# Block 0's residual kept in DRAM through five MLP chunks, with accumulating transfers; down panels not kept split; weight sums spread

## The reference, cut to what matters

```python
h = x + mixed(rms_norm(x)) @ w_out          # RG-LRU and pooling, one input and one output projection
v = rms_norm(h, g_ffn)
up = causal_dwconv(v @ w_up, w_conv_ffn, b_conv_ffn)   # 1024 -> 6144, three taps
gate, val = up[..., :D_FF], up[..., D_FF:]
h = h + (gelu(gate) * val) @ w_down                    # 3072 -> 1024
q = rms_norm(h, g_ple)
h = h + sigmoid(q @ w_ple_gate + b_ple_gate) * (p @ w_ple_proj)
return rms_norm(h, g_final)
```

## Time and profile before

| | us |
|---|---|
| median of three runs | 2188.56 |
| lowest and highest | 2187.64 and 2188.94 |
| the profiled execution | 2192.39 |
| its span | 2190.5 |
| TensorE (PE) busy | 2108.1 |
| VectorE (DVE) busy | 1552.4 |
| ScalarE (ACT) busy | 909.1 |
| GpSimd (POOL) busy, issuing transfers | 396.4 |

### The profile page before, as it was taken

How to read it: one execution, slowest core, us unless ns; L and a number is a source line. 1 busy time by engine, 2 the same in 40 slices (tenths; PEclk the granted TensorE clock), 3 DMA queues, 4 the chain that set the end, 5 groups by cost and what they waited for, 6 DMA issues and landing times.

```text
span 2190.5 us, 24516 instructions
## 1 busy us (share of the span) xinstructions
PE 2108.1 (96%) x9152; PEld 1726.8 (79%) x9152; DVE 1552.4 (71%) x1823; ACT 909.1 (42%) x1194; POOL 396.4 (18%) x720
## 2 busy tenths in 40 slices
PE   8998999898999999898999999999999999999996
PEld 6877877786877778786788888888888888888885
DVE  7884398888888887888888662865555656564866
ACT  5663365253544445354553550641313132323342
POOL 0232322121211111121010010012211111122100
PEclk9999999999999999999999999999999999999998
DMA  5787978766666666668535253556666666666643
GB/s 218 240 235 281 300 239 261 249 238 230 262 230 231 246 245 258 246 237 307 215 107 179 90 204 97 172 174 195 193 192 193 193 194 195 195 193 192 210 155 106
DMA packets 141525, 460.00 MB, mean 210 GB/s; under 512 B 16608, under 2 KB 16736, under 8 KB 139104
## 3 DMA queue, kind: packets, MB, share of 16 engines
q0 software_dynamic: 93120, 350.27, 47.5%
q1 hardware_dynamic: 45984, 99.77, 14.1%
q10 hardware_dynamic: 2304, 8.39, 1.0%
HBM read 279.06 MB, written 204.47 MB: 221 GB/s over the span
## 4 chain that ended last, share of the span: by engine, by line
issue 39%; PE 31%; DVE 16%; POOL 7%; DMA 3%; ACT 2%; SPq 0%; POOLq 0%; DVEq 0%; ACTq 0%
PE slot L788 16%; PE slot L642 15%; POOL wpair L627 7%; DVE H L1874 4%; DVE wpair L1489 3%; DMA raw<-panels 1%; DMA split_panels<-wpair 1%; ACT wpair L923 1%; DVE wsum L1483 1%; DMA XN<-xT 1%; DVE f_quarter L1857 1%; DVE AG L1771 1%; DVE AG L1769 1%; PE slot L706 0%; DVE H L2174 0%
## 5 line engine op out<-in xcount | busy, mean ns | idle before, releaser
L788 PE MATMUL slot<-ops,wpair 128*128 128x512 f32 x3696 | 843.8, 390 | 10.7 <-ACT WG L1202 10.3
L788 PEld LDWEIGHTS slot<-ops,wpair 128*128 128x128 f32 x3696 | 694.2, 188 | 158.3 <-ACT WG L1202 12.9
L853 PE MATMUL slot<-f_quarter,wpair 128*128 128x512 f32 x2016 | 475.1, 396 | 30.4 <-DVE f_quarter L1790 13.9
L853 PEld LDWEIGHTS slot<-f_quarter,wpair 128*128 128x128 f32 x2016 | 383.2, 191 | 120.4 <-issue 35.1
L642 PE MATMUL slot<-Uhi,wpair 128*128 128x512 f32 x1248 | 340.5, 391 | 12.4 <-DVE wpair L1489 10.9
L618 POOL DMA_DIRECT2D split_panels<-wpair x310 | 176.1, 579 | 882.5 <-DVE wpair L1489 861.3
L627 POOL DMA_DIRECT2D wpair<-split_panels x310 | 167.3, 540 | 867.7 <-PE slot L642 348.8
L642 PEld LDWEIGHTS slot<-Uhi,wpair 128*128 128x128 f32 x1248 | 234.5, 188 | 64.1 <-issue 12.6
L1874 DVE TENSOR_TENSOR H<-H,slot 128x512 f32<-128x512 f32 x336 | 214.5, 679 | 38.7 <-PE slot L853 38.2
L923 ACT ACTIVATE wpair<-raw 128x512 fp32r<-128x512 f32 x222 | 135.7, 624 | 224.9 <-PE slot L853 67.6
L642 PE MATMUL slot<-Ulo,wpair 128*128 128x512 f32 x624 | 192.9, 390 | 0.0
(11 more groups left out here) (206 smaller groups left out, 2130.2 us busy)
## 6 DMA issues: line engine op xcount, KB each, us to landing
split_panels<-wpair POOLq DMA_DIRECT2D x310, 512.0 KB, 5.0
wpair<-split_panels POOLq DMA_DIRECT2D x310, 512.0 KB, 3.6
raw<-panels SPq DMA_DIRECT2D x196, 256.0 KB, 4.9
down_sums<-panels POOLq DMA_DIRECT2D x72, 256.0 KB, 8.9
raw<-down_sums SPq DMA_DIRECT2D x48, 256.0 KB, 3.0
H<-xT SPq DMA_DIRECT2D x8, 1024.0 KB, 10.9
pp_kept<-XQ ACTq DMA_DIRECT2D x16, 512.0 KB, 5.6
PPR<-pp_kept SPq DMA_DIRECT2D x16, 512.0 KB, 4.7
```

The lines of the kernel that those rows point to most:

```text
L788: mm = pe.matmul(ps, stat_[:, w], (lo if part else hi)[:, k, :], start=first and k == 0 and i == 0, stop=k == KP - 1 and i == 2, skip_grou ...
L853: mm = pe.matmul(ps, stat_[:, w], f_quarter[:, DOWN_AT[name], part, k, :], start=first and k == 0 and at_pass == 0, stop=k == 1 and at_pas ...
```

## The change

- In block 0, chunks 0 to 4, `H` is not in SBUF. GpSimd stores its eight tiles to `h_acc` in DRAM during the output phase (`h_kept`). The memory of H then holds `FR0` (three raw tiles of f) and ten stages of 128 x 512. Each of a chunk's 28 results is copied from PSUM to a stage, with its sign (`down_staged`): the four of P5 by VectorE with a `tensor_scalar`, the other 24 by ScalarE. GpSimd adds each stage to `h_acc` by an accumulating transfer of 256 KB (`added`). A stage is written again when its transfer of ten before has landed.
- T1 to T4 are then formed from `FR0` as in block 1 (`apart`), T1 as a whole in the chunk's last pair.
- For chunk 5 of block 0 SyncE loads `h_acc` back into `H` after all 140 transfers, between panels of the pair q = 21; that chunk runs as before.
- Down panels are no longer stored split in block 0 (84 of 310). In block 1 GpSimd loads such a raw panel twice, into the high part's place (as fp32r) and into the low part's, and VectorE subtracts one from the other (`raw_lo_part`).
- Stages of the weight sums come after each twelfth panel instead of each fourth.

```diff
-SUM_FIRST, SUM_EVERY = 8, 4
+SUM_FIRST, SUM_EVERY = 8, 12
+STAGES = 10
...
+        if key[1] == "down":
+            RAW_LO[n] = len(RAW_LO) + 1
+            filled[n % RING] += 32
...
+        FR0 = place("FR0", [P, 3, BLOCK], F32, H0)
+        stage = [place(f"stage{i}", [P, BANK], F32, H0 + (3 * BLOCK + i * BANK) * 4) for i in range(STAGES)]
...
+        def apart(b, c):
+            return b > 0 or c < CHUNKS - 1
+        def in_dram(b, c):
+            return b == 0 and c < CHUNKS - 1
...
+                if b == 0:
+                    first = RAW_AT["gate", (CHUNKS - 1) * CHUNK + 1, 0]
+                    panels_to(first)
+                    for i in range(STAGES):
+                        sync.wait_ge(added_in[i], 16 * len(range(i, (CHUNKS - 1) * len(DOWN_STEPS), STAGES)))
+                    sync.wait_ge(d_ready, d_count(0, CHUNKS - 2, "T4"))
+                    for m in range(DT):
+                        sync.dma_start(H[:, m, :], h_acc[m]).then_inc(h_back, 16)
+                        panels_to(first + m + 1)
...
+            def h_kept(m):
+                pool.wait_ge(*out_of((0, "out", m)))
+                pool.dma_start(h_acc[m], H[:, m, :]).then_inc(h_stored, 16)
+
+            def added(c, name, j):
+                g = evicted(c, name, j)
+                row, half, _ = DOWN_OUT[name]
+                ...
+                if name == "P6":
+                    pool.wait_ge(*stage_added(evicted(c, "P3", j)))
+                pool.dma_start(h_acc[j // 2 * 4 + row + j % 2][:, half_of(half)], stage[g % STAGES][:],
+                               accum_op=ALU.add, max_dma_last_dim=ADDED_ROW).then_inc(added_in[g % STAGES], 16)
...
-                pool.dma_start(split_d[n], wpair[n % RING][:].bitcast(F32)).then_inc(split_kept[n % RING], 16)
+                if KEPT_COUNT[n] > (KEPT_COUNT[n - RING] if n >= RING else 0):
+                    pool.dma_start(split_d[n], wpair[n % RING][:].bitcast(F32)).then_inc(split_kept[n % RING], 16)
+                if n in h_behind:
+                    h_kept(h_behind[n])
+                if n in added_behind:
+                    c, name, i = added_behind[n]
+                    if c == 0 and (name, i) == DOWN_ORDER[0]:
+                        pool.wait_ge(h_stored, 16 * DT)
+                    for r in range(2):
+                        added(c, name, 2 * i + r)
...
+                if n in RAW_LO:
+                    pool.dma_start(whi[n % RING], source).then_inc(split_in[n % RING], 16)
+                    pool.dma_start(wlo_raw[n % RING][:], source).then_inc(split_in[n % RING], 16)
+                    continue
...
+            def down_staged(c, name, *js):
+                row, _, column = DOWN_OUT[name]
+                for j in js:
+                    g = evicted(c, name, j)
+                    act.wait_ge(pe_step, STEP[0, "down", c, name, j])
+                    if g >= STAGES:
+                        act.wait_ge(*stage_free(g))
+                    nc.scalar.activation(stage[g % STAGES][:], psum((0, "down", c, j))[:, half_of(column)], ACT.Copy,
+                                         scale=-1.0 if row else 1.0).then_inc(down_signal(c, name, j), 1)
...
+            def raw_lo_part(b, c, *steps):
+                for name, i in steps if b else ():
+                    n = PANEL[b, "down", c, name, i]
+                    dve.wait_ge(split_in[n % RING], IN_COUNT[n])
+                    v.tensor_tensor(wlo[n % RING], wlo_raw[n % RING][:], f32(whi[n % RING]), ALU.subtract
+                                    ).then_inc(raw_lo, 1)
...
                 gate_conv(b, q)
                 refill(b, q, "P4")
                 val_conv(b, q)
+                raw_lo_part(b, c, ("P1", 1))
                 f_tile(b, q)
                 weights(("P1", 0),)
+                raw_lo_part(b, c, ("P5", 1))
+                if in_dram(b, c):
+                    down_staged(c, "P5", 0, 1)
+                    f_lo_tile(b, q)
+                    weights(("P5", 0),)
+                    d_formed(b, c, "T2")
+                    ...
```

More of the change, by code:

```diff
@@ L241 @@
 SPLIT = PANEL[1, "L", 0, 0]
[L245 removed]
+KEPT_AT, IN_COUNT, KEPT_COUNT, RAW_LO = {}, {}, {}, {}
 def kept_panels():
@@ L253, in kept_panels @@
         KEPT_AT[n] = PANEL[(0, *key[1:])]
-        filled[n % RING] += 16
-        IN_COUNT[n] = filled[n % RING]
+        if key[1] == "down":
+            RAW_LO[n] = len(RAW_LO) + 1
+            filled[n % RING] += 32
+        else:
+            filled[n % RING] += 16
+        IN_COUNT[n] = filled[n % RING]
+    stored = [0] * RING
+    for n in range(SPLIT):
+        if PANEL_RAW[n] is None or RAW_WHAT[PANEL_RAW[n]][0] not in ("down", "sum"):
+            stored[n % RING] += 16
+        KEPT_COUNT[n] = stored[n % RING]
 kept_panels()
@@ L342, in build @@
         wsum = place("wsum", [P, PANEL_COLS])
+        wpair0 = at
         wpair = [place(f"wpair{i}", [P, 2, PANEL_COLS], F32R) for i in range(RING)]
+        wlo_raw = [place(f"wlo_raw{i}", [P, PANEL_COLS], F32, wpair0 + (2 * i + 1) * 4 * PANEL_COLS) for i in range(RING)]
         whi, wlo = ([pair[:, part, :] for pair in wpair] for part in range(2))
@@ L373, in build @@
         split_in = [sem(f"split_in{i}") for i in range(RING)]
+        raw_lo = sem("raw_lo")
+        h_stored, h_back = sem("h_stored"), sem("h_back")
+        added_in = [sem(f"added_in{i}") for i in range(STAGES)]
         sum_terms, sum_s1_s3, sum_s2, sum_s4 = sem("sum_terms"), sem("sum_s1_s3"), sem("sum_s2"), sem("sum_s4")
@@ L1337, in pair @@
                 hi(n0 + 6)
-                if b == 0 and q % CHUNK in (1, 2):
+                if not apart(b, q // CHUNK) and q % CHUNK in (1, 2):
                     t1_hi(b, q - 1)
@@ L1367, in weights @@
                         refill(b, "down", c, name, i)
+                if in_dram(b, c):
+                    weights(("P1", 0),)
+                    down_staged(c, "P1", 0, 1)
+                    weights(("P5", 0),)
+                    down_staged(c, "P1", 2, 3)
+                    weights(("P1", 1),)
+                    weights(("P5", 1),)
+                    down_staged(c, "P3", 0, 1)
+                    weights(("P3", 0),)
+                    d_hi_half(b, c, "T2")
+                    down_staged(c, "P3", 2, 3)
+                    weights(("P3", 1),)
+                    d_hi_half(b, c, "T3")
+                    down_staged(c, "P2", 0, 1)
+                    weights(("P2", 0),)
+                    d_hi_half(b, c, "T4")
+                    down_staged(c, "P2", 2, 3)
+                    weights(("P2", 1),)
+                    for name in ("P6", "P7", "P4"):
+                        for i in range(2):
+                            down_staged(c, name, 2 * i, 2 * i + 1)
+                            if (name, i) != ("P4", 1):
+                                weights((name, i),)
+                    return
                 weights(("P1", 0), ("P5", 0), ("P1", 1), ("P5", 1))
@@ L1783, in f_tile @@
                 dve.wait_ge(g_act, b * FT + q + 1)
+                if b == 0 and q == 0:
+                    dve.wait_ge(h_stored, 16 * DT)
                 v.tensor_tensor(f_raw_tile(b, q), AG[:, 0:BLOCK], AV[:, 0:BLOCK], ALU.mult).then_inc(f_raw, 1)
@@ L1852, in d_lo_half @@
                 dve.wait_ge(d_hi, d_count(b, c, name))
-                if b == 0 and name == "T2":
+                if not apart(b, c) and name == "T2":
                     v.scalar_tensor_tensor(d_quarter(name, 1), d_whole(name), -1.0, f32(d_quarter(name, 0)),
@@ L1875, in down_added, with down_staged @@
                                     ).then_inc(signal or slot_free[SLOT[key]], 1)
+            def down_staged(c, name, *js):
+                row, _, column = DOWN_OUT[name]
+                for j in js:
+                    g = evicted(c, name, j)
+                    dve.wait_ge(pe_step, STEP[0, "down", c, name, j])
+                    if g >= STAGES:
+                        dve.wait_ge(*stage_free(g))
+                    v.tensor_scalar(stage[g % STAGES][:], psum((0, "down", c, j))[:, half_of(column)],
+                                    -1.0 if row else 1.0, None, ALU.mult).then_inc(down_signal(c, name, j), 1)
+            def raw_lo_part(b, c, *steps):
[4 more added lines that the diff above has]
+                                    ).then_inc(raw_lo, 1)
             def down_by_seven(b, c, q):
@@ L2062, in pair @@
                 lo(n0 + 5)
-                first_half = b == 0 and q % CHUNK in (1, 2)
+                first_half = not apart(b, q // CHUNK) and q % CHUNK in (1, 2)
                 if follows:
```

131 lines of the change are left out of this document (91 added, 40 removed).

## The result

The changed kernel takes 2338.17 us (median of four runs, 2335.41 to 2342.31) against 2188.75 for the kernel before on the same chip: 1.068 times as long, 95% interval 1.066 to 1.070. That is +149 us where +65 was predicted, outside the range. The page of the kernel after (span, busy us by engine), then its windows (columns as in the earlier trace rows): the five periods from one down phase of block 0 to the next, the last of them, and one chunk of block 1.

A forecast was written before the change was run, and what follows sets the result against it. TensorE, busy for 2108.1 of 2190.5 us, was taken as the bound. Block 0 +43, block 1 +24, early phases -4 and reload +2 gave +65: 2257.4 us profiled, median 2253, range 2180 to 2320.

The forecast's parts named there:

- Engines of block 0: In block 0's down phases, engine gaps fall from 8.8 to 4.7 us per chunk, a gain of 20.5 in five.
- The price of an accumulation: Each accumulating transfer of 256 KB from SBUF into the residual was taken to cost 1.3 us, between 0.65 and 1.5.
- rival 2: Each piece of an accumulating transfer has a fixed price: some 2700 us at 5.2 us, 2370 at 2.2; 10%, above 2330.
- The queue's sum: In GpSimd's queue, 26 accumulations and four stores make block 0's next-pair P4 product 5.5 us too late per chunk.
- The ring hardly binds: In block 0's down phase, with ten stages, waiting for a free stage hardly matters: 28 evictions, at most ten ahead.
- The sums: Full sum stages ahead in block 0's queue add 10.9 us each, a small one 3.3, delaying chunks 0 to 2.
- The reload: In block 0's chunk 5, SyncE's wait for 140 accumulations and eight 512 KB loads cost about +2 us, 0 to 8.
- Block 1: In block 1's down phases, VectorE's new low parts make TensorE wait 4.0 us per chunk, +24 us in six.
- Early phases: Mixing, output and first projections lose 63 of 96 sum transfers and get H's stores: -4 us, between 0 and -9.
- Rival 1: Accumulations in block 0 cost only a copy's price, 0.65 us: +16 in all, 2204 us; 23%, 2190 to 2218.

The follow-up runs named there:

- e5_sums4: The changed kernel with a stage of the weight sums after every fourth panel again, in place of every twelfth; 2301.3 us.
- e2_rawpanels: The kernel before with only the down panels not stored split in block 0 and read raw, twice, in block 1; 2211.0 us, ratio 1.0097.
- e1_sums12: The kernel before with only the stages of the weight sums after every twelfth panel in place of every fourth; 2221.2 us, ratio 1.0140.
- e7_price: A kernel of bare transfers through GpSimd's queue, all computation left out, one kind after another; accumulations of 256 KB in 2 KB rows took 2.90 us each.

## Why the prediction was wrong, step by step

- **Engines of block 0: right.** The gap before P3 is 2.77 in chunk 4 (3.0 predicted); without the adding chunk 3 takes 118.9 (114.2 + 4.7), 4.2 less than before, with its one gap in the place foretold. Only that chunk shows it undisturbed, so the 20 us for five are not shown as a whole.
- **The price of an accumulation: the step that failed.** 1.3 taken, bounded by 0.65 and 1.5; it is 1.7. The upper bound came from transfers in pieces of 8 KB, and rival 2, which saw that rows of 2 KB could cost more, gave it only 10%. The queue's sum itself holds (the prediction wrote 5.5 where its terms give 5.7): with 1.7 it reads (26 x 1.7 + 4 x 1.29)/0.8 + 12.3 + 1.6 + 2.2 = 77.8 against 59.1, 18.7 us late per chunk in place of 5.5; e5_sums4 shows 19 to 22 (138 to 141 against 118.9). Over five chunks that is +66 of the +84 missed: the prediction's own sum would have given about 2320 with 1.7, 18 us short of the measured time.
- **"The ring hardly binds": wrong, by the same price.** 1.7/0.8 = 2.1 us per result against TensorE's 1.36 (six of the 504 matmuls that take 114.24 us in block 1); 70 of 120 evictions waited. This is the mark that the prediction gave for rival 2 and its 2370 at 2.2 us: the truth lay between forecast and rival. The same sum with 2.2 gives about 2400 and not 2370, and 2.2 is not halfway between 1.3 and 5.2.
- **The sums: right in kind, in size by luck.** 36 us predicted beyond the 5.5 per chunk (10.9, 21.8, 3.3), 37 measured by the medians. But by period it is 18, 19 and 9, or 46, in two profiled executions that lie 4.1 above and 2.0 below their medians. For chunk 0 the full stage at panel 68 was left out, for chunk 2 the four transfers at panel 152, both two panels ahead of the down phase.
- **The reload: mis-sized.** 2 us predicted, bound 8, measured 6.5 on e5_sums4 by moving it a pair later, 9 by the periods there and 5 in the kernel after: SyncE's wait is for the last accumulation, and that was 28 us behind TensorE, which follows from the price again.
- **Block 1: right.** 4.0 per chunk predicted and 4.07 measured, 2.94 of it in three gaps (0.60, 1.30, 1.04), the rest shown as busy time; 21 us by e2_rawpanels. **Early phases:** -4 predicted, -5.1 in the table, but the reason is not shown: e5_sums4, with the sums as in the kernel before, begins chunk 0's down phase only 1.0 us later than the kernel after, and 4.1 earlier than the kernel before.
- **Rival 1 did not come true:** an accumulation does not come at a copy's price. Alone in the queue it takes 1.65 to 1.85 us of the engines, a plain store 0.71 to 0.73.

Not predicted at all: that the spread sums also harm the kernel before (e1_sums12, +31).

## What to carry to other kernels

Price an accumulating transfer with its own row length before building on it: here the adding about doubled the bytes' time (1.2 us against 0.65 for 256 KB) and the 128 rows cost some 0.5 more. So this kernel's residual would belong in DRAM only where the queue has well over twice a copy's time to spare (1.7 against 0.65). Ask of each wait in an in-order queue what stands behind it: SyncE's wait for the last accumulation, GpSimd's for a landed stage, and a store behind eight sum transfers were worth 6 to 37 us each. A chunk with a mean DMA share of 0.66 was not free for the sum stages moved into it, since its buffers come free just in time: e1_sums12 lost 13.4 us in chunk 0 and 15.7 in chunk 1.

## What the runs showed of the hardware that was not expected

- The engines' part of a plain store of 128 rows of 2 KB is 0.71 to 0.73 us, of an accumulating one 1.65 to 1.85; with 8 KB rows 1.35 per 256 KB.
- With 1024 for the size of GpSimd's descriptor memory, at most seven plain or three accumulating transfers of 128 rows of 2 KB are issued in a row in e7_price before GpSimd stands (3.6 and some 5 us in the rows above); alone in the queue the latter then take 2.9 us each, with 4096 2.0.
- Beside the loads of the other queue nine accumulations take 38.4 us in e7_price, 4.3 each (335.6 to 374 us). From 336 to 372 us the loads have 61.8% of the engines and q0 37.3%, which over the eight that moved is again 1.68 us. Once the loads have ended, the last fifteen take 2.8 each, about as alone.
- In the kernel after they are issued some 2 us apart with the same descriptor memory (15 from 991.57 to 1018.65 us), closer than the 2.9 of e7_price. Why was not looked into.
